# Gated-scan levels: one 128x128 product a block on keys mixed by a ScalarE copy, in place of two products of 64 columns

## What is computed

```python
decay  = exp(where(tril, cum[t] - cum[s], -inf))            # per channel
scores = einsum('bhtd,bhsd,bhtsd->bhts', q, k, decay)
out    = einsum('bhts,bhse->bhte', scores, v)               # plus the carried state
# forward: k_fwd, f_fwd; backward: the same on the flipped sequence with k_bwd, f_bwd; both are added
```

## Time and profile before

| | |
|---|---|
| median of three executions | 2226.23 us (2223.03 to 2228.01) |
| profiled execution | span 2228.8 us from first to last instruction; it is the only figure given for this execution, and what lies around the span is not listed |
| busy share of the span | PE 98%, DVE 55%, ACT 38%, POOL 4% |
| mean granted TensorE clock | 0.991 of 2.4 GHz |

### The profile page before, as it was taken

The page is one execution under the profiler, slowest core; times in us unless marked ns, Lnnn a source line. Parts: engine busy times, 40 slices in busy tenths (PEclk is TensorE's granted clock), DMA queues, the critical chain, the costliest instruction groups (busy, mean ns, idle before and its releaser), DMA issues.

```text
span 2228.8 us, 27122 instructions
## 1 busy us (share of the span) xinstructions
PE 2186.4 (98%) x10104; PEld 1772.8 (80%) x10104; DVE 1226.8 (55%) x1982; ACT 836.4 (38%) x1288; POOL 92.8 (4%) x73
## 2 busy tenths in 40 slices
PE   8999999999999999999999999999998999999998
PEld 7988888777777778878888887888776778888886
DVE  6886876764666444443333355566764454343443
ACT  6432222242333343342222235344576344232333
POOL 2000000010000000010000021000001001000001
PEclk8999999999999999999999999999999999999999
DMA  8655454432222223323333232112222212323332
GB/s 326 212 190 169 170 170 163 158 113 83 69 67 76 76 76 95 95 76 94 99 99 95 95 94 86 39 57 62 72 85 95 76 53 89 104 91 99 95 94 76
DMA packets 65497, 235.79 MB, mean 106 GB/s; under 512 B 7208, under 2 KB 9384, under 8 KB 64624
## 3 DMA queue, kind: packets, MB, share of 16 engines
q1 hardware_dynamic: 61344, 220.90, 31.0%
q0 software_dynamic: 1872, 11.36, 1.5%
q10 hardware_dynamic: 2176, 2.10, 0.3%
HBM read 230.12 MB, written 4.21 MB: 105 GB/s over the span
## 4 chain that ended last, share of the span: by engine, by line
PE 91%; DVE 5%; ACT 3%; issue 1%; DMA 1%; SPq 0%; DVEq 0%; ACTq 0%
PE bank L1906 24%; PE bank L1907 23%; PE bank L1908 23%; PE bank L1943 3%; PE bank L1945 3%; PE bank L1944 3%; PE bank L2233 2%; PE bank L2093 1%; PE bank L2118 1%; DVE wlo L1121 1%; DVE work L1130 1%; PE bank L2104 1%; PE bank L2309 1%; PE bank L2248 1%; PE bank L2421 1%
## 5 line engine op out<-in xcount | busy, mean ns | idle before, releaser
L1906 PE MATMUL bank<-hhi,whi 128*128 128x512 f32 x1504 | 597.6, 397 | 1.4 <-DVE wlo L1121 1.3
L1121 DVE TENSOR_TENSOR wlo<-raw,whi 128x1024 fp32r<-128x1024 f32 (+1 forms) x353 | 428.9, 1215 | 295.2 <-ACT whi L558 292.7
L1907 PE MATMUL bank<-hlo,whi 128*128 128x512 f32 x1504 | 586.1, 390 | 0.0
L1908 PE MATMUL bank<-hhi,wlo 128*128 128x512 f32 x1504 | 585.8, 390 | 0.0
L558 ACT ACTIVATE whi<-raw 128x1024 fp32r<-128x1024 f32 (+1 forms) x353 | 368.3, 1043 | 468.9 <-PE bank L1908 396.9
L1906 PE MATMUL bank<-ghi,whi 128*128 128x512 f32 (+1 forms) x936 | 359.7, 384 | 10.5 <-DVE wlo L1121 5.8
L1907 PE MATMUL bank<-glo,whi 128*128 128x512 f32 (+1 forms) x936 | 355.6, 380 | 0.0
L1908 PE MATMUL bank<-ghi,wlo 128*128 128x512 f32 (+1 forms) x936 | 355.3, 380 | 0.0
L1906 PEld LDWEIGHTS bank<-hhi,whi 128*128 128x128 f32 x1504 | 282.4, 188 | 70.3 <-issue 9.1
L1908 PEld LDWEIGHTS bank<-hhi,wlo 128*128 128x128 f32 x1504 | 282.4, 188 | 59.6
L1907 PEld LDWEIGHTS bank<-hlo,whi 128*128 128x128 f32 x1504 | 282.6, 188 | 58.5 <-issue 2.6
(11 more groups left out here) (289 smaller groups left out, 2037.6 us busy)
## 6 DMA issues: line engine op xcount, KB each, us to landing
raw<-w SPq DMA_DIRECT2D x393, 512.0 KB, 3.6
work<-w SPq DMA_DIRECT2D x12, 512.0 KB, 10.8
raw<-w SPq DMA_DIRECT2D x16, 384.0 KB, 3.1
gated_in<-w SPq DMA_DIRECT2D x4, 512.0 KB, 9.4
xT<-x_t POOLq DMA_DIRECT2D x1, 2048.0 KB, 12.0
kv_hbm<-work POOLq DMA_DIRECT2D x2, 1024.0 KB, 4.7
work<-rows_hbm POOLq DMA_DIRECT2D x4, 512.0 KB, 5.6
work<-kv_hbm POOLq DMA_DIRECT2D x2, 1024.0 KB, 6.4
```

The source lines that it names most:

```text
L1121: nc.vector.tensor_tensor(wlo[v % 2][:, 0:kc * P], raw[u % 4][:, 0:kc * P], whi[v % 2][:, 0:kc * P].bitcast(F32), ALU.subtract).then_inc(w ...
L1906: nc.tensor.matmul(dst, wh[:, ws], hi[:, c, :], start=c == 0, stop=False)
L1907: nc.tensor.matmul(dst, wh[:, ws], lo[:, c, :], start=False, stop=False)
L1908: ins = nc.tensor.matmul(dst, wl[:, ws], hi[:, c, :], start=False, stop=c == kc - 1)
```

## The change

Before, a level makes two products for each of the four blocks: the forward one has `k0` as its stationary operand and moves the 64 late columns of `q_fwd`, the backward one has `k1` and moves the 64 early columns of `q`. After, ACT first writes a mixed key tile `k_mix`, 128x512, with `k0` at the early positions and `k1` at the late ones. PE makes one product for each block: `k_mix` is stationary, and the 128 moving columns are the early ones of `q` and the late ones of `q_fwd`. The level's mask takes the same entries as before.

`k_mix` is the second half-buffer `gate_in[1]`, which nothing else uses in these units. There is one such tile. PE waits for a new semaphore `mixed`. ACT waits for the keys of the level (`decay`); for level 0 it waits for the gates, and for the last level product of the head before.

On DVE the new decays, queries and keys of an item come ahead of its masked copy.

```diff
+        k_mix = gate_in[1]
...
+            def mix_keys(h, z):
+                m = z - 1
+                if m == 0:
+                    act.wait_ge(fk_done, 2 * h + 2)
+                    act.wait_ge(unit_in, 5 * h + 3)
+                    if h > 0:
+                        act.wait_ge(lev_done, ITEMS * (h - 1) + LEVELS + 1)
+                else:
+                    act.wait_ge(decay, EVENTS * h + 3 + m)
+                s, blk, n = hg[h % 2], 1 << m, S >> (m + 1)
+                nc.scalar.activation(view(k_mix[:, 0:1], [2 * blk, n], [blk, 2], [1, blk]),
+                                     early_late(s["k0"], s["k1"], blk, 0, n), ACT.Copy).then_inc(mixed, 1)
...
             for h, units in unit_groups():
                 for sl, v in enumerate(units):
+                    if sl < 4:
+                        mix_keys(h, max(2 * sl, 1))
                     split_next(v)
                     group_values(v - 1)
+                    if 0 < sl < 4:
+                        mix_keys(h, 2 * sl + 1)
...
                 m = z - 1
+                dve.wait_ge(decay, EVENTS * h + 3 + m)
+                update(s, m)
                 if m < LEVELS:
                     dve.wait_ge(lev_taken, (LEVELS + 1) * h + z)
                     nc.vector.copy_predicated(diag, level_mask[:, m, :].unsqueeze(1).to_broadcast([P, NB, P]),
                                               b3).then_inc(lev_taken, 1)
-                dve.wait_ge(decay, EVENTS * h + 3 + m)
-                update(s, m)
...
                     pe.wait_ge(decay, EVENTS * h + 3 + m)
+                    pe.wait_ge(mixed, LEVELS * h + z)
                     blk, n = 1 << m, P >> (m + 1)
                     for a in range(NB):
-                        for dr in range(2):
-                            half = a * P + (blk, 0)[dr]
-                            qq = (q_fwd, s["q"])[dr]
-                            ins = nc.tensor.matmul(view(b[:, half:half + 1], [2 * blk, n], [1, blk]),
-                                                   s[f"k{dr}"][:, a * P:(a + 1) * P],
-                                                   view(qq[:, half:half + 1], [2 * blk, n], [1, blk]), start=True, stop=True)
+                        ins = nc.tensor.matmul(b[:, a * P:(a + 1) * P], k_mix[:, a * P:(a + 1) * P],
+                                               early_late(s["q"], q_fwd, blk, a * P, n), start=True, stop=True)
```

More of the change, by code:

```diff
@@ L309, in build @@
         sig_done, fk_done = sem("sig_done"), sem("fk_done")
+        mixed = sem("mixed")
         lev_done, lev_taken, decay, sc_taken = sem("lev_done"), sem("lev_taken"), sem("decay"), sem("sc_taken")
```

## The result

The changed kernel takes 2264.65 us (median of four executions, 2263.07 to 2267.16). The kernel before, on the same chip, takes 2226.44 us (2223.03 to 2228.01, four). The ratio is 1.0172 [1.0157, 1.0188], 38.2 us slower. The forecast was 2257, its range 2238 to 2270.

What follows compares the result with a forecast made beforehand. PE, busy for 98% of the span, was taken as the bound. Waits 38.5 less products 23.5 gave +15.0 us, the clock +15.6: 2259.4 in the profiled execution, 2257 us as forecast, range 2238 to 2270.

Steps and rivals of the forecast that it cites:

- rival A: Whole kernel: PE waits at even items and the clock falls behind them; 2257 us, range 2247 to 2268, chance 0.66.
- Products: PE's level products: one wide product costs what one narrow did, 0.89 for 1.73 us at 28 levels, 23.5 us less.
- Odd copies: ACT's copies for items 3, 5, 7: ready before PE asks, covered by 12 matmuls and the masked copy's move; no cost.
- Even copies: ACT's copies for items 2, 4, 6: behind the gate functions, so PE waits at twelve places, 38.5 us in all.
- slot 2: Heads 1 to 3: DVE had 0.49 us left, the odd item starts 0.84 earlier, so DVE is 0.35 us late each.
- Copy: One key copy on ACT: 0.62 us long, 0.75 with tail and hand-over; bounds for its length 0.62 and 1.04.
- Clock: PE's clock falls to 1.2 GHz behind each of twelve waits, costing 1.3 us each (between 0 and 1.6), 15.6 us.
- the estimate made from it, 20 us: Clock falls at the twelve waits, priced from the skill's rule and the trace's 3.4 us: 12 x 1.7 = 20 us.
- Sum: Whole kernel: 2228.8 + 15.0 + 15.6 = 2259.4 us in the profiled execution, so 2257 us forecast.

Runs made afterwards that it cites:

- experiment 1: Changed kernel with ACT's copy for items 2, 4 and 6 moved from behind the gate functions to directly ahead of them; 2216.56 us, ratio 0.9958.
- experiment 4: Changed kernel with twelve useless 512-column matmuls on PE ahead of each even level item in heads 1 to 3; 2248.98 us, ratio 1.0104.
- experiment 3: Changed kernel, still waiting for the copies, but with the eight narrow products of before and the copies' output unused; 2288.79 us, ratio 1.0274.

## Why the prediction was right, and what it sized wrongly

It was right: slower, by the waits at even items and a falling clock, rival A. Its own steps:

- **Products: −23.5 forecast, −21.8 measured.** 24 of 28 levels save 0.84 each, as taken from the earlier trace rows; the four of level 0 save 0.41 (1.75 to 1.34). The prediction had bounded the interleaved operand at 0.89 and 1.73 and took the lower end for all levels. That held for blocks of 4 columns and more.
- **Odd copies: nothing forecast, no wait found.** The reason given (12 matmuls cover them) holds for this kernel only because PE waited at the even item; the kernel of experiment 1, without that wait, had up to 1.7 us there. The price "if the cover is gone" was missing from the prediction, and it is most of the 11 us by which the expectation of experiment 1 was too low (7.0 us at the odd items 5 and 7; the one wait of 1.5 us at L2094 is another part; level 0 is none, as that expectation had counted it at 0.4).
- **Even copies: +38.5 forecast.** The profile lists 38.2 in twelve places; a start late by 3.53 of listed idle time is some 0.16 more on the path, as a matmul's modelled end overlaps its successor. 38.2 + 12 x 0.16 = 40.1, less the 0.42 at L2071 and the three of 0.17 that stood there before, is 39.2. The kernel before has more than the 0.17 us in these places (item 2 to item 3 takes 4.79 us there, other levels 4.56), so 39.2 is rather too much. The term was right to 1 us. By place: 1.46 us where item 4 of head 3 was put near 1.5, 2.09 at item 2 of head 0 (1.78 forecast), and 3.4 to 3.5 at the other ten, behind one gate function or four alike; there the forecasts went from 3.2 to 3.9. The 0.35 us that the prediction added for a late DVE in "slot 2" (by the numbering above it is slot 1) don't show in the changed kernel, whose wait before item 4 is 3.5 us in heads 0, 1 and 2 alike; they do in experiment 4 at the full clock, with 1.07 us before item 4 against 0.70 to 0.75 before items 2 and 6.
- **Copy: 0.62 forecast, 0.61 to 0.67 found** at the even items; between its start and PE's stand 0.76 (1415.87 to 1416.63), and 0.81 before item 2, forecast 0.75.
- **Clock: +15.6 forecast; the mis-sized term.** There are three readings of it. What is left of the 38.3 us is 38.3 + 21.8 - 39.2 = 20.9. The windows give 3 x 1.6 + 7 x 2.6 = 23. The traces of experiment 4 give 19.0 for heads 1 to 3, and with the two falls of 1.6 in head 0 it is 22.2. So it was 21 to 23 us in ten falls, some 2.2 us each, in place of twelve at 1.3. The prediction's bound of 1.6 for one came from a single slow stretch of 3.4 us in the trace of before. Seven of the new ones lasted 6.8 us; they did begin in the wait, as it had allowed for, but some 5.5 us of each lay on PE's work. The Trainium skill ("TensorE: Matmul & The Clock Gate", section HAM oscillation — how this bites in real kernels) prices one fall at half the throttled time, and the estimate made from it, 20 us, was nearer than mine; the trace agrees that a slow stretch costs half of what lies on the work (1.6 of 3.4 us, 2.6 of some 5.5), but not that there is one at every wait.
- **Sum.** 2226.4 + 39.2 - 21.8 + 20.9 = 2264.7, and 2264.65 was measured; as the clock's term here is the remainder, this sum can't fail to close. Of the 7.6 us missed, 5 to 7 are the clock and 1.7 level 0; the waits are right to 1 us either way.

What stays open: why the clock held after the 3.53 us of item 4 in head 0, and after 1.78 us at 1743.66 when it had fallen after 1.77 at the same place before. At item 4 of head 0 it held in experiment 4 as well, after 3.52 us, and fell in experiment 3, after 3.45. No run here separates the causes. Nor was an alternative tried in which ACT's copy is done by DVE or POOL.

## What to carry to other kernels

An operand prepared on another engine costs what stands ahead of it in that engine's order, not its own length: here 0.6 us of copy made waits of 3.5 us, and a better place in the same stream turned 38 us lost into 15 us won. When a wait is taken away, read who had been covered by it; the next wait appeared one item later. A wait of the engine that bounds the kernel is to be priced with the clock behind it, here with more than half as much again.

## What the runs showed of the hardware that I had not expected

- A moving operand that changes place at every column took 168 ns for one row of 128 columns (1.34 / 8), a contiguous one 111 to 114 ns; of the two distances tried neither was dearer.
- Equal idle times of TensorE were not followed by the same clock: after 3.53 us it stayed at 2.4 GHz once and went to 1.2 GHz elsewhere, and the low stretch lasted 3.4 us in three places and 6.8 in seven, and took 1.6 and 2.6 us from the loop.
- Matmuls whose results nobody reads, 108 of them put ahead of the waits' end, made the changed kernel 15.7 us faster (2264.65 to 2248.98).
